# One attention stage instead of two in block 1, with fp32 window scores and other PSUM banks

## What is computed

```python
def neighbourhood_attention(q, k, v, k_ctx, v_ctx, rpb):      # "near": 8 heads of k and v
    s_w = jnp.einsum('bjhd,brjchd->bhjrc', q_i, k_w) * scale + bias[None]
    s_c = jnp.einsum('bjhd,bnhd->bhjn', q_i, k_ctx) * scale
    p = jax.nn.softmax(jnp.concatenate([s_w.reshape(...), s_c], axis=-1), axis=-1)
    o = einsum(p_w, v_w) + einsum(p[..., kr * NA_COLS:], v_ctx)
...
def window_attention(q, k, v, k_ctx, v_ctx, sink):            # "window": 2 heads of k and v, a sink
    s_w = jnp.where(valid, jnp.einsum('bqkgd,bskd->bkgqs', q_n, k_n) * scale, -jnp.inf)
    s_c = jnp.einsum('bqkgd,bnkd->bkgqn', q_n, k_ctx) * scale
    p = sink_softmax(jnp.concatenate([s_w, s_c], axis=-1), sink_b)
    o = einsum(p[..., :span], v_n) + einsum(p[..., span:], v_ctx)
```

## Time and profile before

| | us |
|---|---|
| median of 3 runs | 2668.51 |
| the profiled execution | 2667.57 |
| its span in the trace | 2665.8 |
| TensorE busy | 2453.3 |
| VectorE busy | 1514.4 |
| ScalarE busy | 1266.6 |
| layer 0: near, first score to last sum | 284.7 to 335.8 |
| layer 0: window | 342.4 to 391.8 |
| layer 1: near | 917.7 to 949.6 |
| layer 1: window | 954.1 to 985.1 |

### The profile page before, as it was taken

The page is one execution under the profiler, slowest core; times in us unless marked ns, Lnnn a source line. Parts: engine busy times, 40 slices in busy tenths (PEclk is TensorE's granted clock), DMA queues, the critical chain, the costliest instruction groups (busy, mean ns, idle before and its releaser), DMA issues. The chain is left out here.

```text
span 2665.8 us, 46648 instructions
## 1 busy us (share of the span) xinstructions
PE 2453.3 (92%) x17862; PEld 2231.3 (84%) x17862; DVE 1514.4 (57%) x2668; ACT 1266.6 (48%) x1982; POOL 232.1 (9%) x228
## 2 busy tenths in 40 slices
PE   6898779999989789999998999899999989998998
PEld 4677558887777669989987789899899878898998
DVE  4589663344558665555456655655555556566554
ACT  6364652332456464434355455543533555455434
POOL 0023000000003100012100000021021000000220
PEclk8898889999989899999998999999999989999999
DMA  8322022222452125555543234355445442343553
GB/s 322 126 100 72 2 89 96 101 95 83 170 190 95 46 75 180 176 188 177 192 149 129 96 118 159 137 183 186 152 174 189 153 157 87 111 146 140 179 183 111
DMA packets 59959, 367.18 MB, mean 138 GB/s; under 512 B 5872, under 2 KB 17184, under 8 KB 17312
## 3 DMA queue, kind: packets, MB, share of 16 engines
q1 hardware_dynamic: 59664, 365.07, 38.2%
q10 hardware_dynamic: 144, 0.01, 0.0%
HBM read 357.68 MB, written 7.37 MB: 137 GB/s over the span
## 5 line engine op out<-in xcount | busy, mean ns | idle before, releaser
L252 PE MATMUL psum<-x_hi,w_hi 128*128 128x256 f32 (+1 forms) x3456 | 1069.6, 309 | 59.2 <-DVE x_lo L606 21.9
L210 DVE TENSOR_TENSOR w_lo<-ring,w_hi 128x1024 fp32r<-128x1024 f32 x652 | 823.2, 1297 | 495.9 <-ACT w_hi L198 495.7
L253 PE MATMUL psum<-x_lo,w_hi 128*128 128x256 f32 (+1 forms) x3456 | 1051.1, 304 | 0.0
L254 PE MATMUL psum<-x_hi,w_lo 128*128 128x256 f32 (+1 forms) x3456 | 1050.4, 304 | 0.0
L198 ACT ACTIVATE w_hi<-ring 128x1024 fp32r<-128x1024 f32 (+1 forms) x652 | 658.1, 1051 | 300.0 <-PE psum L1609 135.4
L252 PEld LDWEIGHTS psum<-x_hi,w_hi 128*128 128x128 f32 x3456 | 671.6, 194 | 103.0 <-issue 63.0
L253 PEld LDWEIGHTS psum<-x_lo,w_hi 128*128 128x128 f32 x3456 | 672.1, 194 | 24.9 <-issue 1.9
L254 PEld LDWEIGHTS psum<-x_hi,w_lo 128*128 128x128 f32 x3456 | 671.4, 194 | 23.2
L1606 PE MATMUL psum<-h_hi,w_hi 128*128 (+1 forms) x640 | 176.9, 276 | 0.0
L1608 PE MATMUL psum<-h_lo,w_hi 128*128 (+1 forms) x640 | 176.8, 276 | 0.0
L1609 PE MATMUL psum<-h_hi,w_lo 128*128 (+1 forms) x640 | 176.8, 276 | 0.0
(11 more groups left out here) (302 smaller groups left out, 3071.2 us busy)
## 6 DMA issues: line engine op xcount, KB each, us to landing
ring<-wstream SPq DMA_DIRECT2D x327, 1024.0 KB, 4.8
kept_hi<-x_hi SPq DMA_DIRECT2D x1, 2048.0 KB, 6.3
kept_lo<-x_lo SPq DMA_DIRECT2D x1, 2048.0 KB, 12.7
x_hi<-kept_hi SPq DMA_DIRECT2D x1, 2048.0 KB, 8.0
x_lo<-kept_lo SPq DMA_DIRECT2D x1, 2048.0 KB, 12.5
rel_bias<-bias_by_distance SPq DMA_DIRECT2D x2, 1024.0 KB, 7.5
na_bias<-rpb SPq DMA_DIRECT2D x4, 438.0 KB, 6.1
cst<-consts SPq DMA_DIRECT2D x1, 1662.0 KB, 11.6
```

Source lines behind the costliest of these rows:

```text
L210: dve.tensor_tensor(w_lo[:, c % 2, h], ring[:, (c + 2 * i) % RING, h], w_hi[:, c % 2, h].bitcast(F32), ALU.subtract).then_inc(split_done.s ...
L252: pe.matmul(o, w_hi[:, c, w_cols], hi, start=first, stop=False)
L253: pe.matmul(o, w_hi[:, c, w_cols], lo, start=False, stop=False)
L254: return pe.matmul(o, w_lo[:, c, w_cols], hi, start=False, stop=last)
```

## The change

`attend_both` replaces `attend_near` and `attend_window`: one stage whose steps are near's followed by window's. `halve_stage` is gone: window's q and k are wq and wk themselves, in fp32, and one fp32 matmul for each half takes the place of three products. Without `turn_bank` there are now two sets of score banks (columns 0 to 2047) and one pair of banks for turned probabilities (2048 to 3071). Score t waits for the bias of step t-2, and a turn waits for the copy of the turn before it, as well as for its scaled probabilities. SP brings x back when near's last score is done. The probabilities' buffers are near's throughout, so window's rows are named `nk` too. Block 2's attentions keep their banks and waits.

```diff
-            LAG_T, LAG_V, SETS, PROBS, TURNS = 2, 3, 3, 3, 2
+            LAG_T, LAG_V, PROBS, TURNS = 2, 3, 3, 2
...
+                self.SETS = 1 if turn_bank else 2
...
             def turn(self, u, half, a):
-                at = self.turn_bank + 256 * half if self.turn_bank else 1024 * (u % self.SETS) + 512 * half
+                at = self.turn_bank + 256 * half if self.turn_bank else 2048 + 512 * half
...
-                    if self.turn_bank and t:
-                        pe.wait_ge(biased.sem, self.base[biased] + 2 * t)
-                    elif t >= self.SETS:
-                        pe.wait_ge(turned_sb.sem, self.at(turned_sb, t - self.SETS))
+                    if t >= self.SETS:
+                        pe.wait_ge(biased.sem, self.base[biased] + 2 * (t - self.SETS + 1))
                     q, k = u["q"], u["k"]
-                    for qn, kn in ((0, 0), (1, 0), (0, 1)):
+                    products = ((0, 0), (1, 0), (0, 1)) if len(q) == 2 else ((0, 0),)
+                    for e, (qn, kn) in enumerate(products):
                         for half in range(2):
...
                     pe.wait_ge(scaled.sem, self.at(scaled, v))
-                    if self.turn_bank and v:
+                    if v:
                         pe.wait_ge(turned_sb.sem, self.at(turned_sb, v - 1))
...
-        def halve_stage(jobs):
...
+        def attend_both(layer, tok, nq, nv, na_bias, spent, wq, wk, wv):
...
+                near = steps_of(tok, (x_hi[:, 4:8, :], x_lo[:, 4:8, :]), (x_hi[:, 0:4, :], x_lo[:, 0:4, :]), 2,
...
+                window = steps_of(tok, (wq,), (wk,), 4, lambda h, t: wv[:, t, (h // 4) * DH:(h // 4) * DH + DH],
...
+                a = Attention(near + window, lambda pair: (nq, wq)[pair // 4][:, pair % 4, 0:tok],
+                              attention_buffers(st, 2 * S, spent[:].rearrange("p (a b) t -> p a b t", b=2)))
...
+                        sp.wait_ge(scored.sem, a.at(scored, len(near) - 1))
+                        sp.dma_start(x_hi[:, :, 0:tok].bitcast(F32), kept_hi[:, :, 0:tok]).then_inc(stored.sem, 16)
+                        sp.dma_start(x_lo[:, :, 0:tok].bitcast(F32), kept_lo[:, :, 0:tok]).then_inc(stored.sem, 16)
```

More of the change, by code:

```diff
@@ L692, in pe_score @@
                             mm = pe.matmul(self.score(t, half, k[kn].shape[1]), q[qn][r], k[kn][r],
-                                           start=(qn, kn) == (0, 0), stop=kn == 1)
+                                           start=e == 0, stop=e == len(products) - 1)
                     mm.then_inc(scored.sem, 1)
@@ L785, in act_turned @@
                     w, n = bl[-1][1], len(bl) * P
[L786 removed]
+                    at, wide = (self.turn_bank, 512) if self.turn_bank else (2048, 1024)
                     act.activation(self.probT[0:w, v % self.TURNS, :, 0:n],
@@ L810, in act_exp @@
                     act.activation(hi, self.out(pair)[:, 0:hi.shape[1]], ACT.Copy).then_inc(taken_hi.sem, 1)
[L812 to L841, removed]
         def attention_buffers(st, keys, turned_at=None, side="left"):
@@ L1055, in block1 @@
                                              (nq[:, :, 0:tok], x_hi[:, 4:8, 0:tok], x_lo[:, 4:8, 0:tok])])
-                        attend_near(layer, tok, nq, nv, na_bias, nk)
-                    attend_window(layer, tok, wq, wk, wv)
+                        attend_both(layer, tok, nq, nv, na_bias, nk, wq, wk, wv)
                 with ExitStack() as st2:
@@ L1435, in before_zeros, with steps_of @@
             return bass.AP(t.tensor, t.offset + at, [list(t.ap[0]), [zeros - at, 2], [1, 256]])
-        def steps_of(tok, q, k, group, vals, bias, sink):
+        def steps_of(tok, q, k, group, vals, bias, sink, pair0):
             steps = []
@@ L1447, in steps_of @@
                              vals=[[vals(a, t) for t in range(first // P, 4)] for a in h],
-                             at=tile * P, pair=pair, first=True, last=True)
+                             at=tile * P, pair=pair0 + pair, first=True, last=True)
                     if sink:
@@ L1452, in steps_of @@
             return steps
-        def attend_near(layer, tok, nq, nv, na_bias, spent):
+        def attend_both(layer, tok, nq, nv, na_bias, spent, wq, wk, wv):
             with ExitStack() as st:
[L1456 to L1473, removed]
+                near = steps_of(tok, (x_hi[:, 4:8, :], x_lo[:, 4:8, :]), (x_hi[:, 0:4, :], x_lo[:, 0:4, :]), 2,
+                                lambda h, t: nv[:, t, h * DH:h * DH + DH],
+                                lambda h, qt: before_zeros(na_bias[:], (6 * h + 2 - 2 * qt) * GRID_W, NA_COLS),
+                                None, 0)
@@ new lines, in attend_both, with _ @@
+                with nc.Block() as block:
+                    @block.sync
+                    def _(sp):
+                        sp.wait_ge(scored.sem, a.at(scored, len(near) - 1))
+                        sp.dma_start(x_hi[:, :, 0:tok].bitcast(F32), kept_hi[:, :, 0:tok]).then_inc(stored.sem, 16)
+                        sp.dma_start(x_lo[:, :, 0:tok].bitcast(F32), kept_lo[:, :, 0:tok]).then_inc(stored.sem, 16)
+                        sp.wait_ge(stored.sem, stored.n + 32)
+                    @block.tensor
+                    def _(pe):
+                        for t in range(a.length):
+                            a.pe(pe, t)
+                    @block.vector
+                    def _(dve):
+                        for t in range(a.length):
+                            a.dve(dve, t)
+                    @block.scalar
+                    def _(act):
+                        for t in range(a.length):
+                            a.act_turned(act, t)
+                            a.act_exp(act, t)
@@ L1475, in build @@
+                stored.n += 32
         for layer in range(DEPTH):
```

3 lines of the change are left out of this document (added).

## The result

The changed kernel takes 2632.01 us (median of 4 runs, 2629.25 to 2635.71) where the one before takes 2668.0 (4 runs, 2667.2 to 2668.54): ratio 0.9866, 95% interval 0.9851 to 0.9882. The profiled execution took 2634.25.

The account below looks back on a forecast made before the run. TensorE, busy 92% of the span, was taken as the bound. Layer 0 -14.4 and layer 1 -9.8 gave -24.2: 2667.57 to 2643.4, with 0.94 for the median 2644.3 us; range 2640 to 2653.

Parts of the forecast that it names:

- just score 0.90, turn 1.02, sum 1.18: TensorE alone bounds it: Layer 1 attention steps: the 3.10 us step is wholly TensorE's own work, with no wait in steady steps.
- joining, layer 0: Near score 15 to window score 4 shrinks from 26.23 to 13.61 us by sharing one pipeline: 12.6 saved.
- joining, layer 1: Near score 7 to window score 4 shrinks from 26.22 to 16.18 us: 10.0 saved.
- banks and waits: Both attentions: near's waits -1.3, two fills -1.0, the 0.43 in each of window's four periods -1.7; -4.0 us.
- fp32 scores: Window's scores: row halves run side by side, 1.07 against 0.90 us for 512 columns, 0.64 against 0.55 for 256.
- single file: Rival: window's fp32 row halves run one after the other, 1.93 and 1.07 us a score; +15.5, 2660 us; 10%.
- its milder form: Rival: second fp32 row half starts with the first's second record, +0.43 and +0.21 a score; +7.7, 2652 us; 10%.
- The 0.43 after a 256 step: Layer 0, once per four-step period: a score's wait for ScalarE's copy goes, 0.43 us; near has three, -1.3.
- The fills: Start of near: turn 1 can start 0.94 us earlier, at half clock; half kept, -0.5 per layer, bounds 0 and -1.5.
- One pair of banks for turned probabilities: A turn's wait for the previous copy costs nothing, fitting by 0.12 us in layer 0 and 0.9 in layer 1.
- Bring-back of x: Two DMAs after near's last score land in 8.0 and 12.5 us, hidden behind window's 43 and 26 us.
- Clock in the joined stage: Clock expected at 1.00 through near and window after the fill; the rival, a clock sinking to 0.50, gave 2697 us, 3%.

Follow-up runs that it names:

- the joined kernel with old banks: Changed kernel with the three old sets of score banks, also taking turned probabilities, and the old waits put back; 2647.31 us, ratio 0.9924.
- the old wait without the second stretch: Changed kernel, its banks kept, with every score from step 3 on waiting again for the copy of three steps before; 2647.9 us, ratio 0.9929.
- score ahead, second run: Repeat of the changed kernel with TensorE's order made turn, score of the next step, sum; 2629.43 us, ratio 0.9851.
- score ahead, first run: Changed kernel with TensorE's order changed from score, turn, sum to turn, score of the next step, sum; 2630.54 us, ratio 0.9859.

## Why the prediction was wrong in size

**The step that failed** is the sentence "just score 0.90, turn 1.02, sum 1.18: TensorE alone bounds it", and with it "0.10 of that is the usual change from sum to score". The 1.18 is the distance between two matmul rows and was taken for work; 0.16 of it was a wait for ScalarE's copy. Here are the rows of layer 1's window before, of ScalarE and of TensorE's weight loads (the value in brackets is idle time and what ended it):

```profile
965.75 1.02 ACT L787 ACTIVATE probT<-psum 128x1024 f32<-128x1024 f32 x1 [2.19 <-PE psum L704]
...
966.83 0.53 PEld L692 LDWEIGHTS psum<-wks,wqs 64*128 64x128 f32 x6 [0.32 <-ACT probT L787]
...
968.86 1.02 ACT L787 ACTIVATE probT<-psum 128x1024 f32<-128x1024 f32 x1 [0.67 <-PE psum L704]
...
969.93 0.53 PEld L692 LDWEIGHTS psum<-wks,wqs 64*128 64x128 f32 x6 [0.33 <-ACT probT L787]
```

The copy ends at 966.77 and 969.88, and the score starts 0.06 and 0.05 later; it is so in every steady step of layer 1, and in three of four in layer 0. The matmul row of the same score shows no idle time: the sum's record, 1.09 long, ends only 0.08 us ahead of the score, and a gap that short is not printed. The rest of the wait lies under the record, for without a wait the next group starts 1.02 after the sum does. The order of the program explains the wait: at iteration t TensorE turns step t-2, sums step t-3 and then needs, for score t+1, the copy of the very turn it has just made. Turn start to score start was 2.20 (364.11 to 366.31); turn and sum alone take 1.02 + 1.02. After the change nothing of ScalarE is left in front of a score; the same rows of layer 1, matmuls and one weight load:

```profile
933.60 1.09 PE L704 MATMUL psum<-cst,prob 128*128 128x128 f32 x8
934.62 1.09 PE L717 MATMUL psum<-nk,wv 128*64 128x128 f32 x16
...
934.73 1.02 ACT L787 ACTIVATE nk<-psum 128x1024 f32<-128x1024 f32 x1 [0.68 <-PE psum L704]
...
935.65 0.30 PEld L692 LDWEIGHTS psum<-wk,wq 64*128 64x128 f32 x4 [0.17 <-issue]
```

The copy now runs until 935.75 and the score starts at 935.65, before its end. The table of waits says the same in sums. Layer 0's attentions before:

```profile
engine line waited for: us in total, times, longest us
PE psum L704 <- DVE prob L762: 8.7, 10, 2.4
...
PEld psum L692 <- ACT probT L787: 5.7, 10, 1.5
PEld psum L692 <- ACT nk L787: 5.5, 9, 1.5
```

and after:

```profile
engine line waited for: us in total, times, longest us
PE psum L704 <- DVE prob L762: 6.6, 8, 1.9
...
PEld psum L692 <- DVE mx L737: 2.0, 8, 0.8
```

The last row is the new wait for the bias: 0.8 once, in the fill, and otherwise 0.17, which a weight load shows here without any wait.

**By its terms:**

| term | forecast | measured |
|---|---|---|
| joining, layer 0 (score 15 to w4) | -12.6 | -13.0 |
| joining, layer 1 (score 7 to w4) | -10.0 | -10.85 |
| near's period, layer 0 | 10.51 | 10.32 |
| window's period, layer 0 | 10.86 | 10.53 |
| near's and window's step, layer 1 | 3.10, 3.27 | 2.94, 3.11 |
| fp32 score, 512 and 256 columns | 1.07, 0.64 | 1.06, 0.69 |
| near score 0 to 7: layer 0, layer 1 | -0.9 (fill and one wait), -0.5 (fill) | -2.5, -4.0 |
| join and fp32 together | -20.2 | -20.8 |
| banks and waits | -4.0 | -11.4 in two stages, -10.6 in one |

- *fp32 scores:* right, to 0.01 for 512 columns and 0.05 for 256. The two row halves run side by side; single file and its milder form are out. (In the prediction's sum for window's second half the 0.18 should be the price of 0.17; it makes 0.01.) The window step of 3.27 held to 0.01 with the old wait in place.
- *The 0.43 after a 256 step:* right, but only part. The same wait took 0.16 in every step of layer 1 (3.10 to 2.94) and in more of layer 0's steps than the one in four that was counted, and hid in the "1.18".
- *The fills:* the mis-sized term beside it. Layer 0's near is 2.5 shorter up to score 7, of which 0.43 is the removed wait of score 7; layer 1's is 4.0 shorter. About half of it is clock: TensorE is at 0.50 for 12.2 us instead of 15.4 in layer 0's near, and layer 1's piece has 0.91 instead of 0.78 (rows above). Two pairs of runs put a size to it, an estimate. In layer 0 the joined kernel with old banks runs the same code as the kernel before and differs in the clock alone, 21.35 against 22.64: 1.3. In layer 1 the old wait without the second stretch takes 20.92 against 22.90: 2.0. The other 1.2 and 2.0 are the wait; in layer 1 a little less, since that run's steps carry the unexplained 0.09. The prediction had kept "the clock's rise stays at its time", with a bound of -1.5 a layer for the whole fill. What moves the rise is not settled: with the wait back in the fill of the changed kernel layer 0's stretch is 15.4 again, but the joined kernel with old banks has the same wait and 12.5.
- *One pair of banks for turned probabilities:* right. Where it is tightest, the copy of turn 4 ends at 337.22 and turn 5 starts at 337.37, so 0.15 are left where 0.12 were forecast. In all of layer 0's stage only two turns wait for a copy, turn 1 for 0.27 and one in the drain for 0.18.
- *Bring-back of x:* right. The DMAs are issued at 326.80 and 327.20 and land 8.4 and 12.9 us later, with the stage running to 374.9.
- *Clock in the joined stage:* right, 1.00 from 297.7 to 374.9. The Trainium skill ("TensorE: Matmul & The Clock Gate", section "A second HAM failure mode: psum-queue depth-cycling") would have it swing; the trace after does not agree with that rule either.
- *Stages outside:* the last one became 2.3 shorter. Its time goes with the us that TensorE spends there at 0.50: 71.9 and 1678.4 (changed), 75.4 and 1679.6 (score ahead, second run), 82.2 and 1680.7 (before), 85.5 and 1681.2 (score ahead, first run). What sets these us was not found. The profiled pair differs by 33.3, the medians by 36.0: 2.2 of the 2.7 between them is that the profiled execution of the changed kernel lies above its median (last section).

Added up, the forecast of 2644.3 lies 12.3 above the measured 2632.0. Of that, 8.0 lie in the attentions: 3.3 are the clock in the fills (the estimates above), and the 4.7 that are left are in the main the misread wait, in the steady steps and the fills. 1.1 lie outside the attentions, and 3.2 between a profiled execution and its median, for which the forecast had added 0.94 and the changed kernel would have needed -2.24. These 4.7 by themselves would have put the time at 2639.6, just under the range's end of 2640.

The range failed because its lower end was built from spreads of terms thought to be known. No case stood for the bound itself being misread, though the profile had the row that would have shown it.

## What to carry to other kernels

Before you write "this engine alone bounds the step", look at the waits on the weight-load rows too: a wait of 0.16 us does not show on the matmul row, partly because a matmul's record reaches past the point where the next group can start (1.09 against 1.02), and "group start to group start" is then work plus wait. The reverse shows it too: if some other engine's instruction ends within 0.05 to 0.1 us ahead of the start, in every step, that engine is in the loop. Where two uses of one bank follow each other in the order of the program, separate banks for the two uses can be worth as much as joining two stages (10.6 to 11.4 us against 11.9 here), and the first microseconds of a stage, at half clock, feel a removed wait most: one wait at step 3 cost 2.0 and 1.0.

## What the runs showed of the hardware

- Two fp32 matmuls of 64 rows, on the upper and lower half of the array, overlap: 1.06 us for 2 x 512 columns and 0.69 for 2 x 256, against 0.90 and 0.55 for three products of rounded operands on both halves.
- Many stretches at 0.50 repeat where nothing is changed: in two profiles of the kernel before 32.5 and 32.4 us in layer 0's attentions, 82.2 and 82.2 after layer 1's; in three of the changed one 71.9 each time after layer 1's. Others do not: ahead of layer 0's attention it was 46.1 and 49.5 in the kernel before, 42.5, 48.8 and 52.4 in the changed one. And the kernel with the score ahead had 85.5 in one profile and 75.4 in another, and 3.4 and 6.7 in layer 1's attention, so a gain of a few us inside a stage can be taken back or doubled by the clock elsewhere.
- The 12 executions of the changed kernel fall into two groups, 2629.3 to 2630.8 (mean granted clock 0.969 to 0.970) and 2634.3 to 2635.8 (0.965 to 0.967), with none between. All profiles fell in the upper group, so where those 5 us lie is open.
